# Two chained transformer blocks: the second block's gate products moved into its attentions

## What is computed

```python
h = rmsnorm_2(x, mix_norm_g[l])
proj = h @ w_in[l]
qa, ka, va, q_lat, kv_lat, k_r, g_a, g_b = jnp.split(proj, IN_OFFSETS, axis=-1)
...
o_a = swa_sink_attention(qa, ka, va, swa_sinks[l])
cq = rmsnorm_2(q_lat, q_norm_g[l])
qb = (cq @ w_uq[l]).reshape(B, S, MLA_HEADS, MLA_QK_DIM)
ckv = rmsnorm_2(kv_lat, kv_norm_g[l])
kvb = (ckv @ w_ukv[l]).reshape(B, S, MLA_HEADS, MLA_NOPE_DIM + MLA_V_DIM)
...
o_b = mla_attention(q_nope, q_rope, k_nope, k_rope, vb)
y = jax.nn.sigmoid(g_a) * (o_a @ w_o_swa[l]) + jax.nn.sigmoid(g_b) * (o_b @ w_o_mla[l])
x = x + y @ w_out[l]
h = rmsnorm_2(x, ffn_norm_g[l])
x = x + (jax.nn.silu(h @ w_gate[l]) * (h @ w_up[l])) @ w_down[l]
```

## Time and profile before

| | us |
|---|---|
| three timed runs: median, lowest, highest | 1321.8, 1318.3, 1325.11 |
| the profiled execution | 1318.3 |
| its span, first to last instruction | 1316.5 |
| mean granted clock of PE, as a share of full | 0.981 |
| PE busy | 1232.8 |
| DVE, ACT, POOL busy | 611.9, 553.5, 540.6 |

### The profile page before, as it was taken

One profiled execution on the slowest core, in us unless ns is written; L12 is line 12 of the kernel. 1 busy time (PEld: TensorE's weight loads), 2 busy tenths in 40 slices (PEclk: granted clock), 3 DMA queues, 4 the chain that ended last, 5 costly groups with the idle time before them and its releaser, 6 DMA issues.

```text
span 1316.5 us, 15934 instructions
## 1 busy us (share of the span) xinstructions
PE 1232.8 (94%) x5982; PEld 1026.1 (78%) x5982; DVE 611.9 (46%) x1455; ACT 553.5 (42%) x983; POOL 540.6 (41%) x276
## 2 busy tenths in 40 slices
PE   6989899999899989699797899999999999999997
PEld 4868688888687778599685778887878888888886
DVE  6589565664406355775959820336322222221003
ACT  5442464466533454444864653333332222232112
POOL 4426654444243424233335734343444444443441
PEclk9999999999899999799898999999999999999999
DMA  7213662202221432132020023323222323232221
GB/s 239 79 32 113 153 184 65 96 1 78 99 96 64 144 112 88 41 130 70 1 81 33 1 104 120 96 97 96 80 81 95 102 91 109 84 117 90 96 96 64
DMA packets 71083, 119.20 MB, mean 91 GB/s; under 512 B 5592, under 2 KB 33112, under 8 KB 70624
## 3 DMA queue, kind: packets, MB, share of 16 engines
q1 hardware_dynamic: 71008, 118.19, 27.8%
HBM read 107.67 MB, written 4.21 MB: 85 GB/s over the span
## 4 chain that ended last, share of the span: by engine, by line
PE 77%; DVE 11%; ACT 4%; issue 4%; POOL 2%; SPq 1%; DMA 1%; DVEq 0%; ACTq 0%; POOLq 0%
PE bank L1512 61%; PE bank L1770 9%; PE bank L1596 3%; PE bank L1563 2%; PE bank L1578 1%; DVE sc L1251 1%; DVE m L1247 1%; DVE yB L1011 1%; ACT sc L753 1%; PE bank L1537 1%; DVE tmp L1309 1%; POOL sc L635 1%; DVE sc L1080 1%; ACT pT L747 1%; POOL mK L657 0%
## 5 line engine op out<-in xcount | busy, mean ns | idle before, releaser
L604 POOL TENSOR_TENSOR w_lo<-w_raw,w_hi 128x2048 fp32r<-128x2048 f32 (+5 forms) x95 | 411.7, 4333 | 646.2 <-ACT w_hi L688 624.1
L1512 PE MATMUL bank<-aH,w_hi 128*128 128x512 f32 x800 | 315.7, 395 | 6.4 <-DVE aL L1321 3.9
L1512 PE MATMUL bank<-aH,w_lo 128*128 128x512 f32 x800 | 312.3, 390 | 0.0
L1512 PE MATMUL bank<-aL,w_hi 128*128 128x512 f32 x800 | 312.3, 390 | 0.0
L688 ACT ACTIVATE w_hi<-w_raw 128x2048 fp32r<-128x2048 f32 (+5 forms) x93 | 166.7, 1792 | 269.5 <-PE bank L1512 179.2
L1512 PEld LDWEIGHTS bank<-aH,w_hi 128*128 128x128 f32 x800 | 151.0, 189 | 38.5 <-issue 8.7
L1512 PEld LDWEIGHTS bank<-aH,w_lo 128*128 128x128 f32 x800 | 150.6, 188 | 31.7
L1512 PEld LDWEIGHTS bank<-aL,w_hi 128*128 128x128 f32 x800 | 150.7, 188 | 28.9
L1512 PE MATMUL bank<-uH,w_hi 128*128 128x512 f32 x256 | 102.0, 399 | 13.4 <-ACT yA L699 4.5
L1512 PE MATMUL bank<-w_hi,aH 128*128 128x512 f32 (+4 forms) x256 | 91.6, 358 | 19.6 <-POOL w_lo L604 9.7
L1512 PE MATMUL bank<-uL,w_hi 128*128 128x512 f32 x256 | 101.3, 396 | 0.0
(11 more groups left out here) (283 smaller groups left out, 1996.1 us busy)
## 6 DMA issues: line engine op xcount, KB each, us to landing
w_raw<-in_w_in SPq DMA_DIRECT2D x24, 1024.0 KB, 5.1
w_raw<-in_w_gate SPq DMA_DIRECT2D x22, 512.0 KB, 3.9
w_raw<-in_w_up SPq DMA_DIRECT2D x22, 512.0 KB, 4.8
w_raw<-in_w_down SPq DMA_DIRECT2D x11, 1024.0 KB, 4.9
w_raw<-in_w_merge SPq DMA_DIRECT2D x8, 1024.0 KB, 4.9
w_raw<-in_w_out SPq DMA_DIRECT2D x8, 1024.0 KB, 5.0
w_raw<-in_w_ple_gate SPq DMA_DIRECT2D x4, 1024.0 KB, 4.9
fK<-kbT SPq DMA_DIRECT2D x24, 128.0 KB, 2.4
```

The lines of the kernel that those rows point to most:

```text
L604: pool.tensor_tensor(out=w_lo[:, c % 2, 0:n], in0=w_raw[:, c % 2, 0:n], in1=w_hi[:, c % 2, 0:n].bitcast(F32), op=ALU.subtract).then_inc(w_ ...
L1512: ins = pe.matmul(o, l, r, start=(kk == 0 and m == 0), stop=(kk == total - 1 and m == 2), skip_group_check=True)
```

## The change

- The weights of `n0`, `n1` come ahead of `uq0`, those of `n2`, `n3` ahead of `za0`; the order behind them is `za0`, `zb0`, `za1`, `zb1`.
- `SIDE` gets `swa: (n0, n1)` and `mla: (n2, n3)`. `swa` goes as block 1's attentions do; its first 8 steps lie between the transposes ahead of it. `mla` has 16 steps between its transposes, then one an iteration up to step 32, one more an iteration from i = 22. All four attentions have two score banks and one output bank.
- `uq0`, `ukv0`, `uq1`, `ukv1` follow each other, with the transposes behind; `ukv` outputs are in banks 4 to 7; ACT and not DVE evacuates `t.mk0`, `t.mk1`.
- The gates get tiles of their own in SBUF. ACT makes eight of their sigmoids at the end of `mla` and eight behind it. `za` and `zb` tiles are multiplied by their gate straight out of PSUM by DVE; ACT doesn't evacuate them. The sum's parts are lists of tiles, `z_hi` and `z_lo`.
- `x` is read back from DRAM behind the load of `za0`'s chunk, ahead of `zb0`'s.
- In block 1, `ahead("ya0")` moves into the loop, behind the fourth `uH` copy. The first side steps of `dsa` move ahead of waits for the `t.qa` evacuations.

```diff
     for i in range(2):
+        unit(f"n{i}", D, 4, [(w2, O2_GA + 512 * i, 512)])
+    for i in range(2):
         unit(f"uq{i}", QR, 3, [("w_uq_2", 384 * i, 384)])
         unit(f"ukv{i}", KVR, 2, [("w_ukv_2", 512 * i, 512)])
-    for n, arr in (("za", "w_o_swa_2"), ("zb", "w_o_mla_2")):
-        for i in range(2):
+    for i in range(2, 4):
+        unit(f"n{i}", D, 4, [(w2, O2_GA + 512 * i, 512)])
+    for i in range(2):
+        for n, arr in (("za", "w_o_swa_2"), ("zb", "w_o_mla_2")):
             unit(f"{n}{i}", WA, 4, [(arr, 512 * i, 512)])
-    for i in range(4):
-        unit(f"n{i}", D, 4, [(w2, O2_GA + 512 * i, 512)])
...
+SIDE = {"fox": ("ga", "qa"), "dsa": ("m0", "m1"), "swa": ("n0", "n1"), "mla": ("n2", "n3")}
...
-SIDE_FIRST, SIDE_ALL, SIDE_FROM = 8, 32, 2
-SIDE_TAIL, SIDE_NEXT = 29, 38
-SIDE_HI, SIDE_LO = (20, 27), (20, 27)
-
-
-def side_count(i):
-
-    done = SIDE_FIRST + min(SIDE_ALL - SIDE_FIRST, max(0, i - SIDE_FROM + 1))
-    return done + 2 * max(0, i - SIDE_TAIL + 1)
-
-
-def side_end(tile):
+SIDE_ALL, SIDE_FROM, SIDE_NEXT = 32, 2, 38
+SIDE_FIRST = {"fox": 8, "dsa": 8, "swa": 8, "mla": 16}
+SIDE_TAIL = {"fox": (29, 2), "dsa": (29, 2), "swa": (29, 2), "mla": (22, 1)}
+SIDE_SPLIT = {"fox": (20, 27), "dsa": (20, 27), "swa": (20, 27), "mla": (12, 19)}
...
+def side_count(name, i):
+
+    first, (start, per) = SIDE_FIRST[name], SIDE_TAIL[name]
+    done = first + min(SIDE_ALL - first, max(0, i - SIDE_FROM + 1))
+    return done + per * max(0, i - start + 1)
...
-            for stage, b in ((".l", (4, 5)[i % 2] if side else (4, 5, 2)[i % 3]), (".t", (6, 7, 3)[i % 3])):
...
         for h in range(H):
-            b = 0 if side else h % 2
-            use[name + ".o"].append((b, count[b]))
-            count[b] += 1
-        if side:
-            fill(SIDE[name][0], [1, 2, 1, 2])
-            fill(SIDE[name][1], [1, 2, 4, 5])
+            use[name + ".o"].append((0, count[0]))
+            count[0] += 1
+        fill(SIDE[name][0], [1, 2, 1, 2])
+        fill(SIDE[name][1], [1, 2, 4, 5])
...
-    fill("uq0", four); fill("ukv0", four); fill("t.mq0", [4, 5, 6, 7])
-    fill("uq1", four); fill("t.mk0", [4, 5, 6, 7])
-    fill("ukv1", four); fill("t.mq1", [4, 5, 6, 7]); fill("t.mk1", [4, 5, 6, 7])
+    for i in range(2):
+        fill(f"uq{i}", four); fill(f"ukv{i}", [4, 5, 6, 7])
+    fill("t.mq0", [4, 5, 6, 7]); fill("t.mk0", [0, 3, 4, 5])
+    fill("t.mq1", [6, 7, 0, 3]); fill("t.mk1", [4, 5, 6, 7])
     attention("mla")
-    for n in ("za0", "za1", "zb0", "zb1", "n0", "n1", "n2", "n3", "wp0", "wp1"):
+    for n in ("za0", "zb0", "za1", "zb1", "wp0", "wp1"):
         fill(n, four)
...
+        sgN0, sgN1, sgN3 = place("sgN0", 115, [P, NB, S]), place("sgN1", 123, [P, NB, S]), place("sgN3", 28, [P, NB, S])
+        sgN2 = place("sgN2", 110.5, [P, S])
+        gates2 = ([sgN0[:, j, :] for j in range(NB)] + [sgN1[:, j, :] for j in range(NB)]
+                  + [sq[:, 0, :], sq[:, 1, :], ssum[:], sgN2[:]] + [sgN3[:, j, :] for j in range(NB)])
...
+        yA2, yB2 = place("yA2", 72, [P, KD, S]), place("yB2", 88, [P, 2, S])
+        zH2, zL2 = place("zH2", 92, [P, NB, S], F32R), place("zL2", 100, [P, NB, S], F32R)
+        z_hi, z_lo = ([t[:, j, :] for t in pair for j in range(NB)] for pair in ((zH2, uH2), (zL2, uL2)))
...
-                if c == UNITS["n0"][0]:
+                if c == UNITS["za0"][0]:
                     wait_emptied(sp_, "mla.o", H - 1)
                     sp_.dma_start(xT[:].rearrange("p k t -> p (k t)"), x_dram).then_inc(x_back, 16)
...
-                    for n, at in enumerate(SIDE_LO if name in SIDE else ()):
+                    for n, at in enumerate(SIDE_SPLIT[name]):
                         if at <= i < at + 4:
                             lo_quarter(UNITS[SIDE[name][1]][0] + n, i - at)
...
-            lo_through(UNITS["kvl"][0] + UNITS["kvl"][1])
+            lo_through(UNITS["n0"][0] + 1)
             scale_rows("swa", sc2)
-            lo_through(UNITS["ukv1"][0] + UNITS["ukv1"][1])
+            lo_through(UNITS["n2"][0] + 1)
...
+
+            def gate_sigmoid(block, q):
+
+                wait_emptied(act, ("m", "n")[block - 1] + str(q // NB), q % NB)
+                t = (gates1, gates2)[block - 1][q]
+                act.activation(t, t, ACT.Sigmoid).then_inc(sg_ready, 1)
...
-                    for n, at in enumerate(SIDE_HI if name in SIDE else ()):
+                    for n, at in enumerate(SIDE_SPLIT[name]):
                         if at <= i < at + 2:
                             hi_half(UNITS[SIDE[name][1]][0] + n, i - at)
                     if name == "dsa" and i > NU:
                         silu((i - NU - 1) // NB, (i - NU - 1) % NB)
-                    if name in SIDE and SIDE_NEXT <= i < SIDE_NEXT + 2:
+                    if name == "mla" and i > NU:
+                        gate_sigmoid(2, i - NU - 1)
+                    if SIDE_NEXT <= i < SIDE_NEXT + 2:
                         hi_half(UNITS[SIDE[name][1]][0] + 2, i - SIDE_NEXT)
...
             for i in range(8):
                 act.wait_ge(u_mul, i + 1)
                 act.activation(uH[:, i, :], tmp[:, i % 2, :], ACT.Copy).then_inc(u_hi_ready, 1)
-            ahead("ya0")
-
...
+                if i == 3:
+                    ahead("ya0")
...
-            hi_through(UNITS["kvl"][0] + UNITS["kvl"][1])
+            hi_through(UNITS["n0"][0] + 1)
             exps("swa", sc2, pT2, oA)
...
-            wait_emptied(act, "t.mk1", 3)
-            hi_through(UNITS["ukv1"][0] + UNITS["ukv1"][1])
+            hi_through(UNITS["n2"][0] + 1)
+            for i in range(2):
+                for j in range(4):
+                    evac(f"t.mk{i}", j, mkT[0:MQK, 4 * i + j, :], src=bank_of(f"t.mk{i}", j)[0:MQK, :])
+            wait_emptied(act, "t.mq1", 3)
             exps("mla", sc2, pT2, oB)
             for i in range(8):
                 o = (oA, oB)[i // 4]
                 act.wait_ge(*att_done("swa" if i < 4 else "mla"))
                 act.activation(uH2[:, i, :], o[:, i % 4, :], ACT.Copy).then_inc(u_hi_ready, 1)
-            mix(None, ("za", "zb", "n"), (yA2, yB2), uH2, sg2, 8, ())
+                if i == 3:
+                    ahead("za0")
+            for q in range(8, 16):
+                gate_sigmoid(2, q)
+            ahead("zb0")
+            for t in range(KD):
+                if t == 3:
+                    ahead("za1")
+                if t == 4:
+                    ahead("zb1")
+                act.wait_ge(z_ready, 8 + t + 1)
+                act.activation(z_hi[t], yA2[:, t, :], ACT.Copy).then_inc(u_hi_ready, 1)
             for j in range(KD):
                 if j % 4 == 0:
                     ahead(f"wp{j // 4}")
...
-                    for j in range(NB if name in SIDE else 0):
-                        if i == side_end(j) + 1:
-                            gate_tile(SIDE[name][0], j, (gA if name == "fox" else sgM[0])[:, j, :])
+                    for j in range(NB):
+                        if i == side_end(name, j) + 1:
+                            gate_tile(SIDE[name][0], j, {"fox": gA[:, j, :], "dsa": gates1[j], "swa": gates2[j],
+                                                         "mla": gates2[2 * NB + j]}[name])
...
+            for j in range(NB):
+                gate_tile("n1", j, gates2[NB + j])
             for i in range(2):
                 for b in range(NB):
                     wait_emptied(dve, f"uq{i}", b)
                 uq4 = uq[i][:, :, :].rearrange("p b (h d) -> p b h d", h=4)
                 rope_blocks(uq4[:, :, :, DH:MQK], 4, 16, "3", rp3)
-                if i == 1:
-                    for j in range(4):
-                        evac("t.mk0", j, mkT[0:MQK, j, :], src=bank_of("t.mk0", j)[0:MQK, :])
-                    wait_emptied(dve, "t.mk0", 3)
-                    for h in range(2):
-                        split_head(h)
                 for b in range(NB):
                     splits[0] += 1
                     dve.wait_ge(split_hi, splits[0])
                     src = bank_of(f"ukv{i}", b)[:].rearrange("p (h d) -> p h d", h=4)
                     empties(dve.tensor_tensor(out=mvS[:, 1, b, 4 * i:4 * i + 4, :], in0=src[:, :, DH:2 * DH],
                                               in1=mvS[:, 0, b, 4 * i:4 * i + 4, :].bitcast(F32), op=ALU.subtract), f"ukv{i}", b)
+            for i in range(2):
                 for j in range(4):
                     evac(f"t.mq{i}", j, mqT[0:MQK, 4 * i + j, :], src=bank_of(f"t.mq{i}", j)[0:MQK, :])
-            for j in range(4):
-                evac("t.mk1", j, mkT[0:MQK, 4 + j, :], src=bank_of("t.mk1", j)[0:MQK, :])
+                if i == 0:
+                    wait_emptied(dve, "t.mq0", 3)
+                    wait_emptied(dve, "t.mk0", 3)
+                    for h in range(2):
+                        split_head(h)
             wait_emptied(dve, "t.mk1", 3)
...
             for i in range(8):
+                if i >= 4:
+                    gate_tile("n3", i - 4, gates2[3 * NB + i - 4])
```

(48 more changed lines are left out.)

47 lines of the change are left out of this document (24 added, 23 removed).

## The result

The changed kernel takes **1308.3 us** (median of 4, 1303.9 to 1308.8) against 1322.7 us for the kernel before on the same chip, a ratio of 0.990 (95% interval 0.988 to 0.992). It is faster by 14.4 us, and not by the 25.3 of the forecast's sum; it lies 1.3 us above the range of 1287 to 1307. The profiled execution took 1308.8 us, its span 1307.0.

The account below looks back on a forecast made before the run. PE bounds the kernel, so only its stalls, half clock and small work can go. Block 2's gain of 27.8 us less block 1's 2.5 gives 25.3 off 1318.3: 1293.0, taken as 1296 for a median, range 1287 to 1307.

Parts of the forecast that it names:

- Step 5: Block 2's branch and output products: 43.6 us each, plus 0.5 us (range 0 to 4) for late `zb0` weights.
- Step 4: `mla`: 32.6 us for 48 side steps, 40.9 of its own, 2.5 (0 to 8) toll of GpSimd's queue: 76.0 us.
- Rival C: GpSimd paces `mla`, side steps lengthen each head's loop, 6 to 8 us more, `zb0` late by 2 to 4: 1304 to 1308; chance 0.18.
- Step 2: `swa`: 5 us hole for `n0`'s low half, 1.7 of half-clock loss, 38.1 for 56 side steps, 27.2 of its own.
- The model's own time for `swa`: `swa` without side steps, scaled from block 1's `dsa`: 27.2 us in place of 37.1.
- Step 3: Latent products in one run, then transposes alternating with 16 side steps, up to `mla`'s start: 44.3 us.
- Step 1: Ahead of `swa`: eight side steps (5.4 us) fill PE's holes and delay the first score by only 1.1 us.
- Step 6: Block 1's earlier `ya0` rounding: GpSimd's low half holds up a DVE difference, `ya1` starts later; loss 2.5 us (+3.5 to −4.5).
- B: Block 1's early low half hardly holds DVE up: +3.5 us in place of −2.5, total 1290 us; chance 0.17.
- D: Side steps fill nothing in the attentions, and with two score banks tiles wait for DVE's reduce: slower, 1344 us; chance 0.03.
- E: The gate products are not hidden in the attentions, but nothing new is lost: 1317 us, the same; chance 0.02.

Follow-up runs that it names:

- pieces: Changed kernel with GpSimd's low halves of the first chunks of `ya0`, `ya1`, `za0`, `zb0` made in four pieces each: 1302.8 us.
- The six edits: Changed kernel with `ya0` rounded late, `n3` gates before `uL2`, `x` later, `n0` rounded earlier, `n3` quarters on other rows, `swa` side steps from unit 5: 1290.2 us.

## Why the prediction was right or wrong

**Step 5 failed**, by 5.9 us. It asked only when `zb0`'s weights would be ready, and there it was right: the low half was done 8.8 us behind the last side step (forecast 8.5), and the difference `uL2` of tile 4 came out 9.4 us behind it. It did not go on to ask what stands behind this difference on DVE: `n3`'s gate, and behind the gate a bank that `za0`'s third tile needs. The range of 0 to 4 us was for another wait. With the gates first and `x` later the stretch is 106.8 us, 0.4 us under the forecast, and the 0.5 counted for `zb0` is not there.

**Step 4 was right in its mechanism and wrong in its size.** PE's own work was sized well: 74.57 us busy against 73.5. The toll on top was put at 2.5 us and measured 6.9 (80.4 − 73.5), with PE idle for 5.8 us, 4.2 of them for the split of `mK`. Rival C had the reason for more. The count that was missing: rows 12 to 15 and 19 to 22 each carry a quarter of 1.28 us on top of the earlier trace rows's scales and splits, and a quarter was priced but not the row that it fell on. Other rows for the same quarters give 3.6 of the 4.4 us back.

**Step 2** was 3.0 us short. The hole at the start was forecast at 5 us, with its cause, and measured 4.1. The half-clock stretch that begins in it was counted at 3.4 us and is 6.8 in every kernel that has the hole. Three waits for row scales (1.8 us) were not in the sum either. Together these make 1.5 us (73.0 to 73.2 in six traces); how it divides is not shown. The other 1.5 is a third such stretch that five of the eleven traces with `swa` unchanged, that of the changed kernel among them, show at 680 to 683 us. The model's own time for `swa`, 27.2 us, is nearly reached once the hole and these waits are gone: 66.7 less 38.1 for the steps is 28.6, where the changed kernel has 36.4 and the kernel before 36.9.

**Step 3** was right: 44.2 us in the traces without a half-clock stretch there (forecast 44.3), 45.7 with one. **Step 1** missed by 0.2.

**Step 6** was right in its links: the operation of 5 us, `ya1` at 348.5, 2.6 us later than with the late rounding. That the difference is held for all of GpSimd's pass was the step's price, and trace and pieces bear it out: 5.06 us beside 5.01, 1.79 beside a piece. By the Trainium skill ("SBUF — State Buffer", section "Who interferes with whom") the later of the two blocks and doesn't share; the trace agrees. But between the two traces that the forecast compares the loss does not show (144.3 us in both), as the half clock fell otherwise. That is luck, 2.5 us in the forecast's favour.

**The sum** was made against an execution that had no half-clock stretch in its first 143.2 us; the same code took 143.6 to 149.3 us in the other traces, 0 to 10.2 us of it at half clock. The 3.5 us added for the median cover that. Trace against trace the forecast was 1293.0 and the measurement 1308.8: 15.0 us in block 2 and 3.2 ahead of the first score, less the 2.5 of block 1. Of the 15.0, two ordering waits are 5.9 + 4.4, `swa` 3.0 and the latent products 1.4, and the last two hold a half-clock stretch each that about half of the traces lack. The six edits that cut these waits, none of which changes what is computed, end at 1290.2.

**The rivals.** C's sum, 1304 to 1308, has the result 0.3 us above its upper end, with chance 0.18. Half of it was GpSimd's pace in `mla`, as it said, though in three waits and not in most heads. Its other half, `zb0` late by 2 to 4, did not come; the transfer ahead of `zb0`'s weights was the head of a chain that ended in another wait. B fell with step 6. D and E fell by their totals, 1344 and 1317, and D's waits for DVE's reduce come to no more than 1.0 us in both attentions. But in `swa` taken alone E is close to what happened: 36.4 us of own time (34.9 at equal half-clock time) against 36.9 before, where the forecast's sum has 33.4. No rival had this for one attention alone.

## What to carry to other kernels

When matmuls of a later stage are hidden inside an earlier one, their PSUM banks become the link between the two: list for each bank which instruction frees it, and what stands ahead of that instruction in its engine's program, including work that waits for something else. A helper engine's load has to be added up row by row where it falls, not as a mean over the stage; here the same quarters cost 3.6 us more on one choice of rows than on another. And cutting a wait in front of one product was worth nothing where the next product's weights hung on the same engine (`yb0` behind `ya1`). To see whether work is hidden, compare what a stage grew by with what the added work takes by itself: PE was busy over nine tenths of `swa` in the changed kernel, and the stage had still hidden only 0.5 us of 38.1 (2.0 at equal half-clock time).

## What the runs showed of the hardware

A VectorE difference of two SBUF tiles, 0.68 us alone, takes 5.06 us when it starts inside a GpSimd pass of 5.01 us over SBUF; a gate with one input in PSUM keeps its 0.68 beside a GpSimd piece. GpSimd loses too where VectorE's operations with two SBUF inputs fall between its pieces: four of them took 6.84 us, 1.7 each, where a quarter of the same size takes 1.29 (788.79 in `mla`) and the undivided instruction 4.55 to 5.01. The half-clock stretches come and go in code that is the same: two of them at 26.8 and 81.4 us in the changed kernel's trace, none before 344 us in that of the kernel before. What one costs depends on where it falls: behind `ya1`, where PE seldom waits, 9.6 us of it in place of 3.4 cost 2.9 us (128.5 and 125.6), and beside the waits ahead of `ya1` 6.8 us of it cost nothing (18.9 us with and without). Beside them the first transfers land at other times: six traces with no half clock in the first stretch have it at 143.2 to 145.9 us, and PE waits 9.7 us for the first low half in the kernel before and 10.4 in the one with `x` later, in the same code:

```profile
PE bank L1512 <- POOL w_lo L604: 9.7, 1, 9.7
```

```profile
PE bank L1569 <- POOL w_lo L613: 10.4, 1, 10.4
```

The two together move the first stretch of a single trace by up to 6 us, as much as any one edit did. So only stretches in which PE loses the same to the half clock could be compared to half a microsecond.
